# Cross attention and odd mixer: key and value projections at other places beside the norms, and attention that waits per head and bank

## The reference

```python
def _memory_cross_attention(h, mem_h, w_q, w_kv, q_norm_g, k_norm_g, w_o):
    q = _rms(_split_heads(h @ w_q, 4), q_norm_g)               # 512 tokens, 4 heads of 256
    mk, mv = _split_cols(mem_h @ w_kv, (1024, 1024))           # 256 tokens of memory
    mk = _rms(_split_heads(mk, 4), k_norm_g)
    p = softmax(q @ mk.T * 256 ** -0.5)
    return _merge_heads(p @ _split_heads(mv, 4)) @ w_o

def _odd_mixer(h, w_in, q_norm_g, k_norm_g, rel_bias, w_out):
    q, k, v = _split_cols(h @ w_in, (1024, 1024, 1024))        # 512 tokens, 8 heads of 128
    q, k = _rms(heads(q), q_norm_g), _rms(heads(k), k_norm_g)
    # causal attention, three dilated branches merged, a bias by distance
    return _merge_heads(_dilated_attention(q, k, heads(v), rel_bias)) @ w_out
```

## Time and profile before

| | |
|---|---|
| time, median of 3 runs (lowest, highest) | 3887.62 us (3885.95, 3887.77) |
| the profiled execution: time, span of the trace | 3888.73 us, 3886.9 us |
| TensorE busy, mean granted clock | 3440.9 us, 0.941 |
| VectorE, ScalarE busy | 1553.7 us, 1246.1 us |
| loads, share of 16 DMA engines | 25.7% |
| cross attention of layer 0: lane and norms, then attention | 449 to 523 us, 523 to 559 us |
| odd mixer: lane and norms, then attention from | 1045 to 1176 us, 1176 us |
| cross attention of layer 1: lane and norms, then attention | 1356 to 1430 us, 1430 to 1467 us |

### The profile page before, as it was taken

How to read it: one execution, slowest core, us unless ns; L and a number is a source line. 1 busy time by engine, 2 the same in 40 slices (tenths; PEclk the granted TensorE clock), 3 DMA queues, 4 the chain that set the end, 5 groups by cost and what they waited for, 6 DMA issues and landing times.

```text
span 3886.9 us, 39392 instructions
## 1 busy us (share of the span) xinstructions
PE 3440.9 (89%) x16668; PEld 2752.5 (71%) x16668; DVE 1553.7 (40%) x2049; ACT 1246.1 (32%) x1755; POOL 1.2 (0%) x6
## 2 busy tenths in 40 slices
PE   6886889999988889999879788899999789679998
PEld 5765777878766777887548566788878257557876
DVE  3743344442335334443461463311234732433223
ACT  3314433232344343222351252311122521232222
POOL 0000000000000000000000000000000000000000
PEclk9998989999999989999989999899999999579999
DMA  3211312332310222332541302122121721023332
GB/s 119 66 61 54 98 65 76 98 98 84 114 63 14 76 87 66 98 98 87 189 159 60 60 1 66 44 66 66 55 71 60 261 79 45 1 65 87 98 99 81
DMA packets 326959, 313.81 MB, mean 81 GB/s; under 512 B 22320, under 2 KB 250032, under 8 KB 326520
## 3 DMA queue, kind: packets, MB, share of 16 engines
q1 hardware_dynamic: 326208, 309.14, 25.7%
q10 hardware_dynamic: 576, 2.16, 0.2%
HBM read 309.06 MB, written 2.22 MB: 80 GB/s over the span
## 4 chain that ended last, share of the span: by engine, by line
PE 52%; DVE 6%; ACT 3%; issue 1%; DMA 1%; SPq 0%; DVEq 0%; ACTq 0%
PE ps L310 15%; PE ps L311 15%; PE ps L312 15%; DVE w_lo L268 2%; ACT w_hi L258 1%; PE ps L2613 1%; PE ps L2497 1%; PE ps L2474 1%; PE ps L1491 1%; DVE arena L616 1%; DVE hT_lo L628 0%; PE ps L645 0%; PE ps L2116 0%; SPq L2356 0%; DMA arena<-in_ada_w 0%
## 5 line engine op out<-in xcount | busy, mean ns | idle before, releaser
L268 DVE TENSOR_TENSOR w_lo<-raw,w_hi 128x1024 fp32r<-128x1024 f32 (+2 forms) x510 | 591.0, 1201 | 845.2 <-ACT w_hi L258 845.2
L310 PE MATMUL ps<-hT_hi,w_hi 128*128 128x512 f32 (+2 forms) x2320 | 843.3, 363 | 9.5 <-DVE hT_lo L628 5.9
L311 PE MATMUL ps<-hT_lo,w_hi 128*128 128x512 f32 (+2 forms) x2320 | 839.7, 362 | 0.0
L312 PE MATMUL ps<-hT_hi,w_lo 128*128 128x512 f32 (+2 forms) x2320 | 838.7, 362 | 0.0
L258 ACT CAST w_hi<-raw 128x1024 fp32r<-128x1024 f32 (+2 forms) x510 | 501.3, 1033 | 721.0 <-PE ps L312 698.5
L310 PE MATMUL ps<-w_hi,hT_hi 128*128 128x512 f32 (+1 forms) x1512 | 603.0, 399 | 106.8 <-DVE w_lo L268 42.9
L311 PE MATMUL ps<-w_lo,hT_hi 128*128 128x512 f32 (+1 forms) x1512 | 598.5, 396 | 0.0
L312 PE MATMUL ps<-w_hi,hT_lo 128*128 128x512 f32 (+1 forms) x1512 | 597.9, 395 | 0.0
L310 PEld LDWEIGHTS ps<-hT_hi,w_hi 128*128 128x128 f32 (+1 forms) x2320 | 437.9, 189 | 82.6 <-issue 12.0
L311 PEld LDWEIGHTS ps<-hT_lo,w_hi 128*128 128x128 f32 (+1 forms) x2320 | 438.0, 189 | 68.8 <-issue 1.4
L312 PEld LDWEIGHTS ps<-hT_hi,w_lo 128*128 128x128 f32 (+1 forms) x2320 | 437.7, 189 | 68.2
(11 more groups left out here) (315 smaller groups left out, 3305.2 us busy)
## 6 DMA issues: line engine op xcount, KB each, us to landing
raw<-in_ffn_w_in SPq DMA_DIRECT2D x88, 512.0 KB, 5.1
raw<-in_ada_w SPq DMA_DIRECT2D x24, 1024.0 KB, 5.2
arena<-in_ada_w SPq DMA_DIRECT2D x24, 1024.0 KB, 5.2
raw<-in_ffn_w_gate SPq DMA_DIRECT2D x44, 512.0 KB, 4.0
raw<-in_ffn_w_up SPq DMA_DIRECT2D x44, 512.0 KB, 5.2
raw<-in_ffn_w_out SPq DMA_DIRECT2D x20, 1024.0 KB, 5.0
raw<-in_ffn_w_down SPq DMA_DIRECT2D x20, 1024.0 KB, 5.0
raw<-in_ev_w_in SPq DMA_DIRECT2D x16, 1024.0 KB, 5.4
```

Source lines behind the costliest of these rows:

```text
L268: ins = dve.tensor_tensor(lo[:, half], self.raw_chunk(c)[:, half], hi[:, half].bitcast(F32), ALU.subtract)
L310: pe.matmul(out, w[0], x[0], start=first, stop=False)
L311: pe.matmul(out, w[0], x[1], start=False, stop=False)
L312: return pe.matmul(out, w[1], x[0], start=False, stop=last)
```

## The change

- `head_norm` takes a `pace`: where in the lane's span each engine stands when it comes to four heads, in place of a share a head. It returns the marks of the scaled heads.
- Cross attention: the query norm covers lane positions 2 to 8.9 instead of 2 to 8; the key norm 9 to 12 instead of 8.5 to 12, with the paces shown.
- Odd mixer: `od_bias` runs before the query norm over positions 0 to 1 instead of after the key norm over 13 to 16; the query norm covers 1 to 8.9, the key norm 10 to 16.
- `pipeline` leaves behind by what each bank becomes free.
- `attention_across` has no join; TensorE waits for each head's scaled keys, for each bank's last reader, and before the first product with the values for the copies of the values.

```diff
@@ pipeline
+    for g in range(n):
+        k.bank_free[banks[g % nb]] = (s_dve_freed if owner(g) == "dve" else s_act_freed)(before(g + 1, owner(g)))
@@ head_norm, tensor
         for h in range(nh):
-            k.share("pe", (h + 1) / nh)
+            if not pace:
+                k.share("pe", (h + 1) / nh)
+            elif h % 4 == 0:
+                k.share("pe", pace["pe"][h // 4])
@@ head_norm, scalar
-                k.share("act", (h + 1) / nh)
+                if not pace:
+                    k.share("act", (h + 1) / nh)
+            if pace:
+                k.share("act", pace["act"][n4])
             if ready and n4:
                 k.join(act, "dve")
             act.wait_ge(*s_sums(4 * n4 + 4))
@@ head_norm, vector
             if h % 4 == 0:
-                k.share("dve", (h + 4) / nh)
+                k.share("dve", pace["dve"][h // 4] if pace else (h + 4) / nh)
                 dve.wait_ge(*s_rr(2 * (h // 4) + 2))
@@ head_norm, end
+    return [s_done(per * (h + 1)) for h in range(nh)]
@@ attention_across, tensor
-        k.join(pe, "pe", "dve", "act", "pool")
...
             if u >= 2:
                 pe.wait_ge(*s_pt(u - 1))
+            else:
+                k.wait_bank(pe, 2 + u)
...
             pe.wait_ge(*s_pt(u + 1))
+            for mark in values if u == 0 else ():
+                pe.wait_ge(*mark)
+            for c in range(chunks):
+                if it == 0 and h < sets:
+                    k.wait_bank(pe, obank(h, c))
...
                 if u >= 2:
                     pe.wait_ge(*read(u - 1))
+                else:
+                    k.wait_bank(pe, u)
+                if u % TX == 0:
+                    pe.wait_ge(*ready[units[u][0]])
@@ memory_attention
-    lane.span = (2, 8)
+    lane.span = (2, 8.9)
     head_norm(k, f"xaqn{l}", ...)
-    lane.all_to(8.5)
-    lane.span = (8.5, 12)
-    head_norm(k, f"xakn{l}", ...)
+    lane.all_to(9)
+    lane.span = (9, 12)
+    scaled = head_norm(k, f"xakn{l}", ..., pace={"pe": [1 / 3], "act": [0.5], "dve": [0.5]})
@@ odd_mixer
-    lane.all_to(1)
-    lane.span = (1, 8)
+    q_marks = [q_ready(h) for h in range(8)]
+    lane.span = (0, 1)
+    pipeline(k, "od_bias", ...)
+    lane.all_to(1)
+    lane.span = (1, 8.9)
     head_norm(k, "odqn", ...)
-    lane.all_to(8.5)
-    lane.span = (8.5, 13)
-    head_norm(k, "odkn", ...)
-    lane.span = (13, 16)
-    pipeline(k, "od_bias", ...)
+    lane.all_to(10)
+    lane.span = (10, 16)
+    scaled = head_norm(k, "odkn", ..., pace={"pe": [1 / 3, 2 / 3], "act": [0.4, 0.4], "dve": [0.4, 0.7]})
```

More of the change, by code:

```diff
@@ L1065, in head_norm @@
 def head_norm(k, name, heads, w, dim, gain, scale_log=None, center=False, gate=None, sq=None, rr=None, ready=None,
-              gate_ready=None):
+              gate_ready=None, pace=None):
     nh = len(heads)
@@ L1290, in _, with attention_across @@
                 copy_pt(u - 2)
-def attention_across(k, name, units, nk, scores, table, v_of, chunks, bufs, first):
+def attention_across(k, name, units, nk, scores, table, v_of, chunks, bufs, first, ready, values):
     L, Pb, PT, diag = bufs
@@ L2097, in memory_attention @@
                               lane=lane, banks=(4, 5, 6, 7))
-    project_token(k, f"xav{l}", W[f"xa_v{l}"], 2, lambda i, t: mv[:, t - TX, i * BANK:(i + 1) * BANK],
+    v_ready = project_token(k, f"xav{l}", W[f"xa_v{l}"], 2, lambda i, t: mv[:, t - TX, i * BANK:(i + 1) * BANK],
                   list(range(TX, TALL)), lane=lane, banks=(4, 5, 6, 7))
@@ L2105, in memory_attention @@
               ready=lambda h: sum((q_ready(m) for m in heads[h]), []))
-    lane.all_to(8.5)
-    lane.span = (8.5, 12)
-    head_norm(k, f"xakn{l}", [[mk[:, m] for m in h] for h in heads], SIDE, SIDE,
+    lane.all_to(9)
+    lane.span = (9, 12)
+    scaled = head_norm(k, f"xakn{l}", [[mk[:, m] for m in h] for h in heads], SIDE, SIDE,
               lambda h, i: k.col(f"xak{l}", i), sq=sq, rr=lambda n: rr2,
-              ready=lambda h: sum((k_ready(m) for m in heads[h]), []))
+              ready=lambda h: sum((k_ready(m) for m in heads[h]), []),
+              pace={"pe": [1 / 3], "act": [0.5], "dve": [0.5]})
     lane.end()
@@ L2120, in memory_attention @@
                      lambda h, kt, c: mv[:, kt, (2 * h + c) * P:(2 * h + c + 1) * P], 2, (None, Pb, PT, diag),
-                     W[f"xa_o{l}"])
+                     W[f"xa_o{l}"], scaled, sum((v_ready(c, t) for c in range(2) for t in range(TX, TALL)), []))
     out_project(k, f"xao{l}", W[f"xa_o{l}"], None, KD)
@@ L2219, in odd_mixer @@
                               banks=(4, 5, 6, 7))
-    project_token(k, "odv", W["od_v"], 2, lambda i, t: v[:, t, i * BANK:(i + 1) * BANK], list(range(TX)), lane=lane,
+    v_ready = project_token(k, "odv", W["od_v"], 2, lambda i, t: v[:, t, i * BANK:(i + 1) * BANK], list(range(TX)), lane=lane,
                   banks=(4, 5, 6, 7))
-    lane.all_to(1)
-    lane.span = (1, 8)
-    head_norm(k, "odqn", [[q[:, h]] for h in range(8)], SEQ, P, lambda h, i: k.col("odq"),
-              scale_log=k.eps[:, 2:3], sq=L, rr=lambda n: rr[:, 4 * n:4 * n + 4], ready=q_ready)
-    lane.all_to(8.5)
-    lane.span = (8.5, 13)
-    head_norm(k, "odkn", [[kk_[:, h]] for h in range(8)], SEQ, P, lambda h, i: k.col("odk"),
-              sq=L, rr=lambda n: rr2 if n == 0 else rr[:, 0:4], ready=k_ready)
-    lane.span = (13, 16)
+    q_marks = [q_ready(h) for h in range(8)]
+    lane.span = (0, 1)
     pipeline(k, "od_bias", HEADS8,
@@ L2234, in odd_mixer @@
              owner=lambda g: "dve", banks=(0, 1, 2, 3))
+    lane.all_to(1)
+    lane.span = (1, 8.9)
+    head_norm(k, "odqn", [[q[:, h]] for h in range(8)], SEQ, P, lambda h, i: k.col("odq"),
+              scale_log=k.eps[:, 2:3], sq=L, rr=lambda n: rr[:, 4 * n:4 * n + 4],
+              ready=lambda h: q_marks[h])
+    lane.all_to(10)
+    lane.span = (10, 16)
+    scaled = head_norm(k, "odkn", [[kk_[:, h]] for h in range(8)], SEQ, P, lambda h, i: k.col("odk"),
+              sq=L, rr=lambda n: rr2 if n == 0 else rr[:, 0:4], ready=k_ready,
+              pace={"pe": [1 / 3, 2 / 3], "act": [0.4, 0.4], "dve": [0.4, 0.7]})
     lane.end()
@@ L2242, in odd_mixer @@
                      lambda h, it: U[:, h, SEQ - P - P * it:SEQ],
-                     lambda h, kt, c: v[:, kt, h * P:(h + 1) * P], 1, (L, Pb, PT, diag), W["od_out"])
+                     lambda h, kt, c: v[:, kt, h * P:(h + 1) * P], 1, (L, Pb, PT, diag), W["od_out"], scaled,
+                     sum((v_ready(c, t) for c in range(2) for t in range(TX)), []))
     out_project(k, "odo", W["od_out"], None, KD)
```

## The result

The changed kernel takes 3843.36 us (median of 4 runs, 3841.48 to 3845.67) against 3887.69 us (4 runs, 3885.95 to 3891.52): a ratio of 0.9885, 95% interval 0.9868 to 0.9902. The forecast was 3844, range 3834 to 3857. The profiled execution took 3842.66 us with a span of 3840.9 us, 46.0 us less than before.

The account below looks back on a forecast made before the run. It took TensorE's stops, and the low clock after them, as the bound. Cross attentions 29.4 us plus odd mixer 14 made 43.4: 3888.73 becomes 3845.3, less 1.1 for the median, forecast 3844, range 3834 to 3857.

Parts of the forecast that it names:

- First stop: Cross attention: TensorE's 7.95 us wait for the low part of value chunk 1 would be gone.
- the new one in front of chunk 2: Cross attention: TensorE would newly wait 3.3 us for value chunk 2's low part, queued behind VectorE's scaling of the queries.
- second stop: Cross attention: TensorE's 7.72 us stop in the join before the scores would be gone.
- the sign of being right: Cross attention of layer 0: first scores straight behind the last value matmul, at about 509 to 511.
- The low clock after the new stop: Cross attention: the 3.3 us stop before value chunk 2 would bring the low clock, costing 2.0 us a layer.
- The odd mixer's 1.7: Odd mixer: low clock after the 3.0 us stop at value chunk 2, as likely there, would cost 1.7 us.
- New stop: Odd mixer: a 3.0 us stop, as value chunk 2 is cast only behind the squares of head 3.
- The wait of the key sums for squares: Odd mixer: the 1.80 us wait of head 4's sums for squares behind Exp would become 0.6 us at two places.
- VectorE's lateness at the attention's start: Odd mixer: the attention's first addition would come about 1.3 us later against the first score than before.
- the rival that they cost: Attention units: the new TensorE waits cost over 0.68 us each, making the kernel slower; at 0.9 us 3902; chance 0.02.
- only the joins fall: All three stages: the moved splits buy nothing, only the joins' removal gains, 29 us, 3859; chance 0.06.
- The table switch: Cross attention: no 1.38 us drain expected; by the skill page queries' scaling would be 1.4 us later, the sum 2.8 smaller.

Follow-up runs that it names:

- The earlier split: Changed kernel with the cross attentions' query norm span ending at 9.1 instead of 8.9, so value chunk 2 is split before the queries' Ln and scaling: 3839.20 us.
- the last three edits: Separately on the changed kernel: cross-attention query span to 9.1, 3839.20 us; odd mixer all_to(10.1), 3841.63 us; odd mixer ScalarE second pace 0.7, 3845.57 us.
- the flips early: Changed kernel with the odd mixer's old lane positions (query norm 1 to 8, key norm 8.5 to 16, a share a head), od_bias still early: 3856.12 us.
- All three edits together: Changed kernel with query span to 9.1 in cross attentions, all_to(10.1) and ScalarE second pace 0.7 in the odd mixer: 3838.03 us, run again 3837.06 us.

## Why the prediction was right

- *Cross attention*: 14.7 us a layer forecast, 14.9 and 15.3 measured. First stop gone; the new one in front of chunk 2 3.12 us (forecast 3.3). The earlier split confirms that the chunk's place in the queues made it. The prediction named VectorE's scaling as the cause; in its own sum the cast from 493 on allows the low part at 496.5 and the scaling at 497.6, so already there two thirds of the stop belonged to the late cast, as in the rows after. Keys scaled well before TensorE is free; second stop gone. The first scores came at 511.74 where 509 to 511 was the sign of being right; the stage began 1.35 us later than before (406.79 against 405.44), and less that they are inside.
- *The low clock after the new stop*: forecast yes, at 2.0 us. It came in both layers, for 3.4 us each, and cost 1.7. The odd mixer's 1.7 stands in the prediction without a row of its own, inside its 1.4 to 2.9; 3.4 us at the low clock behind the stop of 2.93 us cost just that.
- *Odd mixer*: 14 us forecast, 13.0 measured. New stop 2.93 (forecast 3.0), released by VectorE's copy, not by the split. The wait of the key sums for squares (1.80 us before, 0.6 forecast) is gone altogether; the 0.53 us at 1076.12 lies in the query norm, where 0.74 us stood before and nothing was forecast. The mis-sized term is VectorE's lateness at the attention's start: 1.3 us forecast; the first read came 2.9 us after the first score instead of 0.5, so 2.4, and its stop of 2.46 us was followed by the low clock once more, 1.7 us that the sum does not have. In working it out I let Ln of the last four heads begin when their sums end. For these heads the table load stands behind that wait, not in front of it (timeline of ScalarE before and after):

```profile
1141.02 1.28 ACT L1122 ACT_TABLE_LOAD   x1 [4.87 <-PE ps L1095]
```

```profile
1135.66 1.28 ACT L1134 ACT_TABLE_LOAD   x1 [1.26 <-PE ps L1104]
```

  That is 1.3 us for everything after it, on VectorE too. The two misses are 1.1 and 1.7 us, and the stage missed its 14 by 1.0 only, because 1.8 us came that the sum does not name: the key sums' wait that did not come, one wait of 0.6 us fewer in the first units, and less busy time than the clock accounts for. That part of the agreement is luck.
- *The waits*: the rival that they cost did not come; a unit still lasts 2.2 us. That only the joins fall is out (the run without the moves gains 6.3 us, the one with the join 39.8). What the moves give without the new waits is 39.8 of 43.2 us.
- *The table switch*: after the change Ln ends at 487.90, the table load runs from 487.91 for 1.28 us, and Exp starts at 489.21. The drain that the Trainium skill charges beside it (ScalarE: Activation LUTs, section What ACT_TABLE_LOAD costs) shows neither in front of the load nor behind it in this trace.

```profile
485.92 1.98 ACT L1134 ACTIVATE arena<-ps,eps_sb 128x2048 f32<-128x2048 f32 x1 [3.62 <-PE ps L1104]
487.91 1.28 ACT L1139 ACT_TABLE_LOAD   x1
489.21 2.01 ACT L1139 ACTIVATE arena<-arena,eps_sb 128x2048 f32<-128x2048 f32 x1
```

- *The total* agrees better than it deserves by the stages: 43.4 forecast and 43.2 measured there, with the cross attentions 0.8 us over and the odd mixer 1.0 under, while 46.0 between the two profiled spans contain 3.9 us of clock behind and some 1 us lost ahead of the stages. The medians are 44.3 apart.

What stays open: why the window behind grows when the stages shrink further. In the five profiles with the changed order of the cross attention and none of the last three edits (the changed kernel twice, the join put back, the cross attentions alone, the flips early) it lasts 2353.5 to 2354.6 us; in the five profiles with one or all of these edits 2357.0 to 2361.3 us, in the four with the old cross attention 2354.4 to 2357.9 us, the idle time being the same to 1.6 us. The medians agree: each of these kernels is 2 to 7 us slower than its stages say. That is more regular than chance of single executions would suggest, but the kernel before differs from itself by 3.4 us there, and no run shows what decides it. All three edits together remain the fastest kernel measured, 1.3% below the kernel before.

## What to carry to other kernels

When work of one engine is interleaved by hand into waits of another, look at what is queued *behind* the wait on every engine: the long stop before was a split that stood behind an Exp it had nothing to do with. A wait for everything can be left in place if the last thing it waits for is hidden; removing it without the moves gave 6 us, moving the work without removing it gave 40. Compare stages between the same instructions, since the total carries several us of clock from stretches that no edit touches.

## What the runs showed of the hardware

Stops of TensorE of 3.12 and 2.93 us were followed by 3.4 us at the low clock in every profile, as were those of 2.46 us in four of five profiles (6.8 us in the fifth). Of six stops of 2.23 or 2.24 us four left the clock at full and two did not, the same kernel doing both. In the windows behind, the idle time of all fourteen profiles lies within 246.2 to 247.8 us, while TensorE's busy time for the same instructions ranges from 2106.7 to 2114.1 us. That spread, 7 us of 3840, is larger than several of the edits tried here.
